# Band attention on one Trainium2 core: taking its 32 items in pairs of heads

## The reference, cut to what matters

```python
sc = jnp.einsum('bqhd,bkhd->bhqk', qi, kb).astype(jnp.float32) * scale + bias[None]
sc = jnp.where(valid[None, None, None, :], sc, NEG)
p = jax.nn.softmax(sc, axis=-1)
return jnp.einsum('bhqk,bkhd->bqhd', p.astype(vb.dtype), vb)
```

## Time and profile before

| | |
|---|---|
| Time, median of 3 runs | 1760.69 us (1760.42 to 1760.83) |
| Profiled execution, its own time | 1760.4 us |
| Its span, first to last instruction | 1758.6 us |
| PE busy | 1692.0 us, 96% |
| DVE busy | 867.5 us, 49% |
| ACT busy | 625.7 us, 36% |
| POOL busy | 645.0 us, 37% |
| Mean granted clock of TensorE | 0.981 |

### The profile page before, as it was taken

The page is one execution under the profiler, slowest core; times in us unless marked ns, Lnnn a source line. Parts: engine busy times, 40 slices in busy tenths (PEclk is TensorE's granted clock), DMA queues, the critical chain, the costliest instruction groups (busy, mean ns, idle before and its releaser), DMA issues.

```text
span 1758.6 us, 20419 instructions
## 1 busy us (share of the span) xinstructions
PE 1692.0 (96%) x8117; PEld 1337.1 (76%) x8117; DVE 867.5 (49%) x1225; ACT 625.7 (36%) x1014; POOL 645.0 (37%) x290
## 2 busy tenths in 40 slices
PE   6999999999999989999999998999989899999997
PEld 5877666678986767778877786787777688888886
DVE  5336565476333643333335636454475576262624
ACT  6534334364433432222222343462233332222222
POOL 3432222244741333334433333232144254444441
PEclk9999999999999999999999999999999899999998
DMA  7222211242541267863332224221034233333331
GB/s 223 84 84 62 60 49 43 65 121 84 168 120 36 73 212 233 266 217 89 98 109 86 79 71 140 71 61 48 25 108 132 60 105 99 96 96 96 96 96 60
DMA packets 295474, 181.21 MB, mean 103 GB/s; under 512 B 8129, under 2 KB 279267, under 8 KB 295124
## 3 DMA queue, kind: packets, MB, share of 16 engines
q1 hardware_dynamic: 291388, 170.50, 32.4%
q10 hardware_dynamic: 3432, 7.29, 1.2%
q0 software_dynamic: 560, 2.12, 0.3%
HBM read 174.09 MB, written 5.79 MB: 102 GB/s over the span
## 4 chain that ended last, share of the span: by engine, by line
PE 93%; DVE 3%; ACT 1%; issue 1%; DMA 1%; ACTq 0%; POOL 0%; SPq 0%; DVEq 0%
PE ps L1085 61%; PE ps L1097 13%; PE ps L1111 5%; PE ps L1273 2%; PE ps L1241 1%; PE ps L1411 1%; PE ps L1355 1%; PE ps L1253 1%; PE ps L1336 1%; PE ps L1232 1%; PE ps L1161 1%; PE ps L1590 1%; DMA raw<-in_w_in_dram 0%; PE ps L1556 0%; PE ps L1430 0%
## 5 line engine op out<-in xcount | busy, mean ns | idle before, releaser
L557 POOL TENSOR_TENSOR WL<-raw,WH 128x1024 fp32r<-128x1024 f32 (+2 forms) x282 | 642.5, 2280 | 1078.1 <-ACT WH L580 1078.0
L580 ACT ACTIVATE WH<-raw 128x1024 fp32r<-128x1024 f32 (+2 forms) x282 | 281.7, 1000 | 815.9 <-PE ps L1085 683.1
L1085 PE MATMUL ps<-hH,WH 128*128 128x512 f32 (+1 forms) x800 | 203.1, 396 | 5.3 <-DVE tmp L1733 5.1
L1085 PE MATMUL ps<-hL,WH 128*128 128x512 f32 (+1 forms) x800 | 198.1, 390 | 0.0
L1085 PE MATMUL ps<-hH,WL 128*128 128x512 f32 (+1 forms) x800 | 197.6, 389 | 0.0
L1085 PEld LDWEIGHTS ps<-hH,WH 128*128 128x128 f32 (+1 forms) x800 | 148.4, 188 | 43.5 <-issue 11.6
L1085 PEld LDWEIGHTS ps<-hL,WH 128*128 128x128 f32 (+1 forms) x800 | 150.0, 187 | 32.4
L1085 PEld LDWEIGHTS ps<-hH,WL 128*128 128x128 f32 (+1 forms) x800 | 149.5, 187 | 31.8
L1097 PE MATMUL ps<-hH,WH 128*128 128x512 f32 x328 | 137.9, 420 | 0.7 <-DVE vfTc L2090 0.7
L1097 PE MATMUL ps<-hL,WH 128*128 128x512 f32 x328 | 129.1, 394 | 0.0
L1097 PE MATMUL ps<-hH,WL 128*128 128x512 f32 x328 | 129.1, 394 | 0.0
(11 more groups left out here) (470 smaller groups left out, 2670.8 us busy)
## 6 DMA issues: line engine op xcount, KB each, us to landing
raw<-in_w_in_dram SPq DMA_DIRECT2D x64, 512.0 KB, 3.7
raw<-in_w_mlp_dram SPq DMA_DIRECT2D x64, 512.0 KB, 3.9
ada_w<-in_w_ada_dram SPq DMA_DIRECT2D x48, 512.0 KB, 5.7
raw<-in_w_gate_up_dram SPq DMA_DIRECT2D x44, 512.0 KB, 5.7
raw<-in_w_out_dram SPq DMA_DIRECT2D x16, 512.0 KB, 3.7
raw<-in_w_ckv_dram SPq DMA_DIRECT2D x16, 512.0 KB, 3.8
raw<-in_w_down_dram SPq DMA_DIRECT2D x16, 448.0 KB, 3.4
raw<-in_k_dft_dram SPq DMA_DIRECT2D x17, 256.0 KB, 2.7
```

The lines of the kernel that those rows point to most:

```text
L557: pool.tensor_tensor(WL[un.slot][:, 0:s_.kt, 0:n], raw[un.slot][:, 0:s_.kt, 0:n], WH[un.slot][:, 0:s_.kt, 0:n].bitcast(F32), ALU.subtract) ...
L580: act.activation(WH[un.slot][:, 0:s_.kt, 0:n], raw[un.slot][:, 0:s_.kt, 0:n], ACT.Copy).then_inc(high_done, 1)
L1085: ins = pe.matmul(dst, w[un.slot][:, q, 0:m], a[:, q, :], start=(k == 0), stop=(k == 3 * kt - 1))
```

## The change

Band items are numbered in another order: item n of the band belongs to pair n // 8, query tile n % 8 // 2, and within the pair to head n % 2. Two neighbouring items are the same query tile of two heads that share a tile of q and k.

- PE issues both scores of such a pair in the even step, one behind the other, on row halves 0 to 63 and 64 to 127, each with its own increment of `scored`; the odd step issues none. The pair waits until the maximum of the item two before its first is taken (before, each item waited for the one three before it).
- The weighing is done for two heads at once, four times (after steps 26, 34, 42 and 50) in place of eight. Its matmuls alternate between the two column halves of bank 2.
- The waits that count weighed heads count pairs from then on: ACT's copy of item n >= 1 waits for the weighing of the pair before (or of the last differential head), and DVE's copy out waits for the pair.
- The order of everything else stays: maxima, exponentials, normalisations, transposes and copies still go item by item, one per step.

```diff
         def item(g):
-            return ("a", g) if g < A_ITEMS else ("b", g - A_ITEMS)
+            if g < A_ITEMS:
+                return "a", g, g // ST, g % ST
+            n = g - A_ITEMS
+            return "b", n, n // 8 * 2 + n % 2, n % 8 // 2
...
             def keep_ab(m):
...
-                if kind == "b" and h >= 1:
-                    act.wait_ge(pv_done["ab"], A_HEADS + max(h - 1, 0))
+                if kind == "b" and n >= 1:
+                    act.wait_ge(pv_done["ab"], A_HEADS + n // 8)
...
             def score_ab(g):
...
-                    if n < 3:
+                    if n == 0:
                         pe.wait_ge(exped["ab"], A_ITEMS)
                     else:
-                        pe.wait_ge(maxed["ab"], g - 2)
-                    rows = slice(64 * (h % 2), 64 * (h % 2) + 64)
-                    ins = pe.matmul(bank(3 + n % 3, nk), qB[rows, h // 2, q], kB[rows, h // 2, 0:nk],
-                                    start=True, stop=True)
+                        pe.wait_ge(maxed["ab"], g - 1)
+                    for e in range(2):
+                        rows = slice(64 * e, 64 * e + 64)
+                        ins = pe.matmul(bank(3 + (n + e) % 3, nk), qB[rows, h // 2, q], kB[rows, h // 2, 0:nk],
+                                        start=True, stop=True)
+                        if e == 0:
+                            ins.then_inc(scored["ab"], 1)
                 ins.then_inc(scored["ab"], 1)
...
+            def weigh_b(p):
+                pe.wait_ge(kept["ab"], A_ITEMS + 8 * (p + 1))
+                if p:
+                    pe.wait_ge(out_b, p)
                 else:
...
+                    pe.wait_ge(out_a, A_HEADS)
                 for b in range(ST):
-                    ins = pe.matmul(ps[rows, 2, b * P:S], v[:, b, c], src[:, b, b * P:S],
-                                    start=(b == 0), stop=True, skip_group_check=True)
+                    for e in range(2):
+                        c = (2 * p + e) * B_DH
+                        ins = pe.matmul(ps[64 * e:64 * e + 64, 2, b * P:S], vB[:, b, c:c + B_DH], attB[e][:, b, b * P:S],
+                                        start=(b == 0), stop=True, skip_group_check=True)
                 ins.then_inc(pv_done["ab"], 1)
...
-                if g < AB:
+                if g < A_ITEMS or g < AB and g % 2 == 0:
                     score_ab(g)
...
-                if m >= ST and m % ST == 1 and g < STEPS - 1:
-                    weigh_ab(m // ST - 1)
+                if m >= ST and m % ST == 1 and m // ST <= A_HEADS:
+                    weigh_a(m // ST - 1)
+                if m > A_ITEMS and (m - A_ITEMS) % 8 == 0:
+                    weigh_b((m - A_ITEMS) // 8 - 1)
...
                 elif head % 2:
-                    dve.wait_ge(pv_done["ab"], head + 1)
+                    dve.wait_ge(pv_done["ab"], A_HEADS + (head - A_HEADS) // 2 + 1)
                     dve.tensor_copy(qB[:, (head - A_HEADS) // 2, :], bank(2)).then_inc(out_b, 1)
```

More of the change, by code:

```diff
@@ L682, in exp_ab @@
             def exp_ab(g):
-                kind, n = item(g)
-                nk, k = (n % ST + 1) * P, 2 * (n % 4)
+                kind, n, h, qt = item(g)
+                nk, k = (qt + 1) * P, 2 * (n % 4)
                 act.wait_ge(maxed["ab"], g + 1)
@@ L699, in keep_ab @@
             def keep_ab(m):
-                kind, n = item(m)
-                h, qt = n // ST, n % ST
+                kind, n, h, qt = item(m)
                 act.wait_ge(turned["ab"], m + 1)
@@ L1251, in turn_ab, with weigh_a @@
                 src = pA[n % 4][:, 0, :] if kind == "a" else pB[n % 4][:]
-                for b in range(n % ST + 1):
+                for b in range(qt + 1):
                     ins = pe.transpose(ps[:, 7, b * P:(b + 1) * P], src[:, b * P:(b + 1) * P], ident[:])
                 ins.then_inc(turned["ab"], 1)
[L1256 to L1263, removed]
-                else:
[L1265 to L1271, removed]
+            def weigh_a(h):
+                pe.wait_ge(kept["ab"], ST * (h + 1))
+                if h:
+                    pe.wait_ge(out_a, h)
+                for b in range(ST):
+                    ins = pe.matmul(ps[:, 2, b * P:S], vA[:, b, h * P:(h + 1) * P], attA[h % 2][:, b, b * P:S],
+                                    start=(b == 0), stop=True, skip_group_check=True)
+                ins.then_inc(pv_done["ab"], 1)
+            def weigh_b(p):
+                pe.wait_ge(kept["ab"], A_ITEMS + 8 * (p + 1))
+                if p:
+                    pe.wait_ge(out_b, p)
+                else:
+                    pe.wait_ge(out_a, A_HEADS)
                 for b in range(ST):
-                    ins = pe.matmul(ps[rows, 2, b * P:S], v[:, b, c], src[:, b, b * P:S],
-                                    start=(b == 0), stop=True, skip_group_check=True)
+                    for e in range(2):
+                        c = (2 * p + e) * B_DH
+                        ins = pe.matmul(ps[64 * e:64 * e + 64, 2, b * P:S], vB[:, b, c:c + B_DH], attB[e][:, b, b * P:S],
+                                        start=(b == 0), stop=True, skip_group_check=True)
                 ins.then_inc(pv_done["ab"], 1)
@@ L1294, in _ @@
                     pe.matmul(bank(6), ones[:], tmp[h][:], start=True, stop=True).then_inc(head_mm, 1)
-                if g == STEPS - 1:
-                    weigh_ab(A_HEADS + B_HEADS - 1)
                 un, part = half_at(g)
```

## The result

The changed kernel takes 1738.83 us (median of 4 runs, 1738.45 to 1739.25) against 1760.56 for the kernel before on the same chip: a ratio of 0.9875, with a 95% interval of 0.9863 to 0.9887. The forecast was 1739.4, in a range of 1735.5 to 1749. The profiled execution took 1739.09 us, its span is 1737.3.

A forecast was written before the change was run, and what follows sets the result against it. TensorE, busy for 96% of the span, was taken as the bound. Terms 11.6 + 9.2 + 2.4 - 1.6 - 0.3 = 21.3 us came off the 1760.7 us median, giving 1739.4, range 1735.5 to 1749.

The forecast's parts named there:

- The twin for the scores: Band scores: a pair costs what a differential score on two row halves does, 2.96 us for four widths; 11.6 us removed.
- The extra increment: Score pair: an increment on the first product too, absent in the differential score; taken as 0, ends 0 and 1 us.
- Column halves: Weighing: two heads' column halves run side by side, 2.30 us a pair, four pairs for eight heads; 9.2 us removed.
- the conditioning product: Block of 32 passes over four column quarters, 1.84 us; four passes cost what one costs, the evidence for side-by-side weighing.
- the serial case: Rival at the weighings: column halves run in series, 4.60 us a pair, nothing saved there; 1748.6 us, chance 7%.
- the partial one: Rival at the weighings: column halves overlap in part, each round baring a 0.14 us weight load; 1743.9 us, chance 9%.
- Changes of shape: Transposes ahead of a tiled score or weighing cost 0.17 us more; 14 fewer such places, 2.4 us removed.
- the halves: Projection matmuls of each step, 2.86 us a block; taken as the same in number, with no saving in the sum.
- The waits: New PE waits: 0.8 us each from head steps 22 and 30, 0.3 from the roots of step 37.
- the waits are worse: Rival: DVE reaches the reciprocals later and ACT is late behind new weighings, 5 us lost, not 1.9; 1742.5 us, 8%.
- the pair's wait decides: Rival at even steps: score pairs wait for DVE's maximum, PE and DVE taking turns; slower than before, 1763.1 us, 2%.
- 2 us to each side: Allowance for the granted clock: a shift may add or spare a 1.2 GHz stretch at the stage's end and later waits.

The follow-up runs named there:

- later reciprocals and roots: Changed kernel with each head step's scaling and reciprocal one step later and the four square roots in step 41, not 37: 1737.32 us, again 1736.96.
- nearer maximum: Changed kernel with each score pair waiting for the maximum of the item just before it, not the one before that: 1744.04 us, one run.

## Why the prediction was right

*The twin for the scores.* The forecast took 2.96 us for the four widths of a pair, from the differential scores; measured are 0.42, 0.63, 0.85 and 1.06, together 2.96, and 11.62 removed for 11.6. The number holds; the reason given with it ("the second row half rides along for nothing") covers 8.5 of it, and the other 3.1 is the fixed part of a block. The step priced a pair by its twin, which holds both, so the sum didn't suffer; the two expectations that took it apart did. The extra increment costs nothing that shows: the pair with two takes as long as its twin with one, where the estimate from the Trainium skill ("TensorE: Matmul & The Clock Gate", per-tile semaphore tail) was 0.4 us for all 16.

*Column halves.* 2.30 us a pair, as the conditioning product implied: 9.16 removed for 9.2. Neither the serial case (4.60) nor the partial one (one load laid bare a round) happened. That the forecast holds rests on the alternation that the change chose: with one head behind the other, 3.0 would have been removed. The efficiency of 0.79 that the Trainium skill ("TensorE: Matmul & The Clock Gate", measured speedup against the span model) shows for three column tiles isn't seen here with two: 16 passes take 2.37 where 8 took 2.37.

*Changes of shape.* 2.37 removed for 2.4 at the transposes. The same change took 0.4 us off the halves, which the sum had at nothing.

*The waits.* Places, cause and order were as worked out: the transposes of steps 24 and 32 behind ACT's copy (0.81 and 0.76 us), and those of step 39 behind the roots (0.27), for 0.8, 0.8 and 0.3. That match flatters the forecast: the listed gaps begin at the modelled end of the last matmul, while the forecast counted PE from block start to block start. Counted like that they are 0.97, 0.95 and 0.41, together 2.3 and not 1.9. What was missing is the time from the copy's end to the first transpose, 0.14 us each time (220.12 to 220.26 in the rows above). The 0.4 that it makes and the 0.4 of the halves cancelled in the sum, which is luck. That all three go with the later reciprocals and roots shows the cause. The rival "the waits are worse" is out, since nothing waits behind the new weighings. So is "the pair's wait decides": with the nearer maximum, a stricter wait, 14 of the 16 pairs still had slack.

*What was outside the sum.* The stage gave 21.2 for 21.3. Around it, +2.0 and -2.1 us cancelled in the profiled run, and that they did is luck too; 2 us to each side had been allowed for that, and it is larger than any error inside.

## What to carry to other kernels

Where matmuls use half the rows or half the columns of TensorE, put the two halves' matmuls next to each other in the stream, or at most a few passes apart, and look for a twin in the same trace to price it: here both kinds had one, and the forecast was within 0.6 us. Count blocks as well as columns, as each change between full and half shape has a price of its own (0.2 us in the block and 0.17 at the transposes ahead of it). When the bound engine gets shorter steps, walk the others through the steps where they have their longest instruction; and price a wait from the release to the first instruction behind it, and with its clock: two waits of 2.9 us in place of two of 0.8 cost 8.5 us more, over half of it by the low clock behind them.

## What had not been expected

- Two heads one after the other still overlap at their seam: 3.86 us where two blocks of 2.30 were expected to add up. A third of the gain on the weighings needs no alternation.
- A part of the gain from pairing can be had without the second row half: two scores on the same rows in one block save 3.1 of 11.6 us, and the transposes behind them 2.3 more.
- PE standing for 2.9 us brought a granted clock of 0.70 to 0.80 in the windows behind it. The same wait of 2.2 to 2.4 us at "up" was followed by a lower clock in five of the ten profiles and not in the other five.
